# Keeping 32 sample rows in four groups of 32 partitions with 256 columns, from w_out to picking

## The chip, the cores and the metric

The kernel runs on one core of a Trainium2 chip. The metric is the device time of one execution in microseconds (us). Shorter is better. The core's engines are TensorE (PE in the profile, its weight loads PEld), VectorE (DVE), ScalarE (ACT), GpSimd (POOL) and SyncE (SP). SP issues nearly all transfers, on one queue; 16 DMA engines carry them out.

## What is computed

One inference step of a one-layer decoder with 256 prompt rows and 32 sample rows (8 sequences of 4) of 1024 columns, all float32. The part around the change:

```python
merged = (jax.nn.sigmoid(gate_a) * (o_a.astype(x.dtype) @ w_branch_a)
          + jax.nn.sigmoid(gate_b) * (o_b.astype(x.dtype) @ w_branch_b))
x = x + merged @ w_out
h = moe(rmsnorm(x, norm2_w).reshape(B * T, D_MODEL), router_w, router_b,
        expert_w_gu, expert_b_gu, expert_w_down, expert_b_down)
x = x + h.reshape(B, T, D_MODEL).astype(x.dtype)
# moe: logits = x @ router_w + router_b; the 4 best of 32 experts a row, softmax over the 4;
# an expert: h = x @ w_gu + b_gu; act = clamp and SwiGLU of h; out = act @ w_down + b_down
```

Then a final norm of the rows. Every expert's weights are 12 MB (`w_gu` 1024 x 2048, `w_down` 1024 x 1024), and all 32 experts are read.

## The kernel before

**Tiles.** `TILES` (L43) splits the 288 rows in two tiles of 128 prompt rows (0 and 1) and tile 2 with the 32 sample rows. `acc(t)` (L326) says where a tile's rows x stand in PSUM: tiles 0 and 1 in two banks each, 128 partitions by 1024 columns; tile 2 in bank 7, where partition group h (32 partitions) holds columns 256h to 256h+255 of the 32 rows. So the sample rows are in four groups there, but norm, transposes, router and picking of the experts' rows take them as 32 partitions by 1024 columns, from `x2[0:32, 2, :]`.

**Order.** The code writes the order of every engine out by hand, with semaphores between them. The stages around the change:

- SP (L438 to L464) loads the router's weights, the residual rows (`x_sample` as four transfers of 32 rows by 256 columns, L446), the first expert's chunks, `norm2_w` over all partitions (L450, after the wait for `merged` 8), biases, further chunks as their places come free: chunk 6 after the router's first part (`x2T` 4, L458), chunk 7 after w_out (`wo_done` 4), chunk 8 after the last logits, and every later one when the chunk that held its place is used (`w_used`, L466). An expert has six chunks of 2 MB; there are 11 places (`FULL`), in the loop 8 (`WS`).
- PE (L1111 to L1159): `w_out_tile` of tile 2, tile 0, the first half of tile 1; transposes of tile 2 (8, each of 32 rows by 128 columns) and tile 0; the second half of tile 1 in parts, and between these the router (`part_logits`, `fold_logits`, `last_logits`); the ranks of the rows in their experts (`rank`, `total`); then the first expert's picking (L1207), its transposes, and the experts. `keep_busy` issues matmuls whose results nobody reads.
- ACT (L1720, `residual_norm`): sums of squares and 1/rms of each tile. For tile 2 it first copies bank 7 to `x2[0:32, 2, :]` (4 copies), then squares two halves.
- DVE (L2213 to L2292): adds x (`add_x`), scales the rows by 1/rms and `norm2_w`, chooses the experts, makes `sel`, a one-hot matrix of rows by 64 slots; after that the tables for all experts.
- POOL (L2517 to L2551): constants: `ramp`, `fold`, the expert biases in bfloat16, and at its end `same_row`, which sums a column over the four groups; it is used for the final norm at L1398.

**Experts.** For each expert PE runs `gate_up` (L1239), `pick` of the next expert's rows (L1162: rows = sel^T x2, six matmuls of 512 columns, the two of tile 2 with 32 rows), transposes and `down` (L1272); every second expert it adds the outputs to `acc` through `add`. `b_down` (L1185) adds the down bias, once.

Of the kernel before, what the change touches and what calls it, by code (L numbers as in the profile page):

```python
# [27 lines left out]
P = 128  # L28
# [8 lines left out]
D = 1024  # L37
# [39 lines left out]
def layer_kernel(nc, x_prompt, x_sample, state_hgrn, state_rwkv, state_shift, norm1_w, w_in, hgrn_lb_logits,  # L77
# [5 lines left out]
    with ctx:  # L83
# [110 lines left out]
        gselc, selc = ltake(2 * TW), st3[:, 15:18]  # L194
# [26 lines left out]
        same_row = before  # L221
        fold, sq_n = inb[:, 0:NE], qk[:, 0:512]
        part = sk[:, 0:P + NS]
# [5 lines left out]
        bdn = x2[:, 2, :]  # L229
# [6 lines left out]
        sel, gsel = fm[11][:, 0:3 * SLOTS], fm[11][:, 256:256 + 6 * SLOTS]  # L236
# [95 lines left out]
        X2_ORDER = (2, 0, 1)  # L332

# [9 lines left out]
        RR, XX, WO = 7, 7, 4  # L343
# [39 lines left out]
        def _(sp):  # L383
# [72 lines left out]
            for x in range(1, 4):  # L456
                sp.dma_start(bdn[NE * x:NE * x + NE, :], expert_b_down[0]).then_inc(S("bdn_loaded"), 16)
# [61 lines left out]
        def _(pe):  # L519
# [558 lines left out]
            def x2_T(t, out, k0=0, k1=KT):  # L1078

                rows = TILES[t][1]  # L1080
                for k in range(k0, k1):
                    b, c = (out[(k - k0) // 4], (k % 4) * P) if t < 2 else (out[0], k * NS)
                    i = nc.tensor.transpose(b[:, c:c + rows], x2[0:rows, t, k * P:(k + 1) * P], ident[0:rows, 0:rows])
                    if k % 4 == 3 and (t < 2 or k == 7):
                        done(i, "x2T")
# [10 lines left out]
            def fold_logits():  # L1096

                for t, c in ((0, 0), (2, P)):
                    rows = TILES[t][1]
                    i = mm(logit_cols(t)[0:rows, :], part[:, c:c + rows], fold, start=True, stop=True)  # L1100
                done(i, "logits")
# [19 lines left out]
            pe.wait_ge(S("ramp"), 1)  # L1121
# [16 lines left out]
            def rank(t, first=False):  # L1138

                n = TILES[t][1]  # L1140
                return mm(bank[1][:, P + t * NE:P + (t + 1) * NE], before[0:n, :], M[0:n, t * NE:(t + 1) * NE], start=first, stop=True,
                          skip_group_check=True)
# [42 lines left out]
            def b_down():  # L1185

                for t, (o, rows) in enumerate(TILES):
                    for h, (out, c) in enumerate(acc(t)):
                        r = 32 * (1 + (2 * t + h) % 3)
                        i = mm(out, wT[r:r + NE, o:o + rows], bdn[r:r + NE, c], start=False, stop=True, skip_group_check=True)  # L1190
                return i
# [13 lines left out]
            pe.wait_ge(S("rstd"), 7)  # L1205
            pe.wait_ge(S("sel_ready"), 1)
            for j, b in enumerate((bank[6], bank[0])):  # L1207
                for t, (o, rows) in enumerate(TILES):
                    for h in range(2):
                        c = h * 512 + j * 256  # L1210
                        i = mm(b[64 * h:64 * h + 64, 0:256], sel[0:rows, t * SLOTS:(t + 1) * SLOTS], x2[0:rows, t, c:c + 256],
                               start=(t == 0), stop=(t == 2), skip_group_check=True)
# [69 lines left out]
            def pe_pair(quad, p):  # L1282
# [4 lines left out]
                for x in range(2):  # L1287
# [21 lines left out]
                    if x == 1 and static and quad == 0 and p == 1:  # L1309
                        pe.wait_ge(S("bdn_loaded"), 48)  # L1310
# [86 lines left out]
            pe.wait_ge(S("ramp"), 2)  # L1397
# [5 lines left out]
        def _(act):  # L1403
# [316 lines left out]
            def residual_norm(t, wo):  # L1720
# [25 lines left out]
            def x2_evac(t, n, b, k0):  # L1746
# [4 lines left out]
                else:  # L1751
                    i = fn(x2v[:, :, NP_:NT], b[:, 0:KT * NS].rearrange("p (k t) -> p k t", k=KT), ACT.Copy)
# [8 lines left out]
            done(fn(part, bank[6][:, 0:P + NS], ACT.Copy), "x2T_evac")  # L1761
            residual_norm(1, (3, 4))
            act.wait_ge(S("rstd"), 6)
# [110 lines left out]
        def _(dve):  # L1874
# [327 lines left out]
            def onehot(out, c0, w, slots, weights=None):  # L2202

                for t, (o, rows) in enumerate(TILES):
                    dst, src, s1 = out[0:rows, t * w + c0:t * w + c0 + SLOTS], ramp[0:rows, 0:SLOTS], slots[0:rows, t:t + 1]
                    if weights is None:
                        i = v.tensor_scalar(dst, src, s1, None, ALU.is_equal)
                    else:
                        i = v.tensor_scalar(dst, src, s1, weights[0:rows, t:t + 1], ALU.is_equal, ALU.mult)
# [3 lines left out]
            dve.wait_ge(S("norm_loaded"), 32)  # L2213

            def norm_rows(n, dst, order):

                for x, t in enumerate(order):
                    rows = TILES[t][1]
                    if n == 1:
                        add_x(t, x + 1)  # L2220
                    dve.wait_ge(S("rstd"), 3 * n + x + 1)
                    for out, c in acc(t) if t < 2 else [(x2[0:rows, 2, 0:512], slice(0, 512)), (x2[0:rows, 2, 512:D], slice(512, D))]:
# [356 lines left out]
```

## Time and profile before

| | us |
|---|---|
| median of 3 runs | 1319.13 (1318.65 to 1320.28) |
| the profiled execution | 1319.96 |
| its span in the profile | 1318.2 |
| PE busy | 1286.8 (98%) |
| DVE busy | 374.7 (28%) |
| ACT busy | 241.9 (18%) |
| POOL busy | 53.4 (4%) |

Times in the profile count from the span's start. An instruction's line is the line of the kernel; all of ACT's `activation` calls have one line, L1405, that of a helper, so they are told apart by shape and time. "arena" and "ring" are the two large SBUF areas, "bank" a PSUM bank.
### The profile page before, as it was taken

The page shows a single profiled execution, that of the slowest core. Times are in us where ns is not written, and L with a number is a line of the kernel's source. Part 1 is how long each engine was busy: PE and PEld are TensorE (multiplying, and loading weights), DVE is VectorE, ACT ScalarE, POOL GpSimd, SP SyncE. Part 2 cuts the span into 40 slices and gives each one's busy share as a digit, 9 for nine tenths or more (in the row PEclk, how much of TensorE's full clock was granted, in tenths as well). Part 3 has the DMA queues.
Part 4 walks back from the last instruction along what each step waited for, and adds up shares of the span by engine and source line. Part 5 has one row for each costly group of instructions (what it writes and reads, how often), then busy time and mean ns, then how long its engine had stood idle before and what let it go on. Part 6 is the DMA issues. An engine that isn't in the chain of part 4 may idle for free.

```text
span 1318.2 us, 18429 instructions
## 1 busy us (share of the span) xinstructions
PE 1286.8 (98%) x7369; PEld 614.9 (47%) x7369; DVE 374.7 (28%) x1017; ACT 241.9 (18%) x532; POOL 53.4 (4%) x129
## 2 busy tenths in 40 slices
PE   9999999999999999999999999999999999998987
PEld 6778778888744333333333333333333323232333
DVE  3234756554327121121211212212112111211112
ACT  3143343222122110111101111111101101110102
POOL 5000200000060000000000000000000000000000
PEclk9999999999999999999999999999999999999999
DMA  7635437001878999999999999999999999999996
GB/s 234 171 100 191 134 85 271 33 33 34 320 263 352 429 429 428 429 429 428 418 430 429 429 430 430 430 430 430 430 430 430 429 430 430 430 430 429 428 429 266
DMA packets 72736, 449.40 MB, mean 341 GB/s; under 512 B 14404, under 2 KB 43126, under 8 KB 47880
## 3 DMA queue, kind: packets, MB, share of 16 engines
q1 hardware_dynamic: 67090, 445.72, 82.7%
q10 hardware_dynamic: 5590, 2.88, 0.7%
q8 instruction: 42, 0.69, 0.2%
q14 instruction: 14, 0.11, 0.0%
HBM read 443.82 MB, written 4.76 MB: 340 GB/s over the span
## 4 chain that ended last, share of the span: by engine, by line
PE 78%; DMA 17%; DVE 2%; ACT 1%; issue 0%; POOL 0%; SPq 0%; DVEq 0%; POOLq 0%; ACTq 0%
PE bank L1258 25%; PE bank L1278 13%; DMA ring<-in_expert_w_gu_dram 7%; PE bank L559 7%; PE bank L649 5%; PE bank L1166 5%; DMA arena<-in_expert_w_gu_dram 5%; PE bank L1197 4%; DMA extra<-in_expert_w_down_dram 3%; DMA extra<-in_expert_w_gu_dram 2%; PE bank L1073 2%; PE bank L1047 2%; PE bank L940 2%; ACT arena L1405 1%; PE bank L1173 1%; PE bank L923 1%
## 5 line engine op out<-in xcount | busy, mean ns | idle before, releaser
L1258 PE MATMUL bank<-arena 128*64 128x512 f32 x960 | 216.6, 594 | 2.2 <-DMA arena<-in_expert_w_gu_dram 2.2
L1405 ACT ACTIVATE arena<-bank 128x512 f32<-128x512 f32 (+6 forms) x232 | 115.2, 515 | 484.0 <-PE bank L1278 195.9
L1258 PE MATMUL bank<-ring,arena 128*64 128x512 f32 x848 | 189.7, 594 | 3.8 <-DMA ring<-in_expert_w_gu_dram 3.8
L1405 ACT ACTIVATE arena<-arena 128x256 f32<-128x256 f32 (+7 forms) x124 | 68.9, 564 | 470.8 <-DVE arena L2353 463.6
L2353 DVE TENSOR_SCALAR arena<-bank 128x256 f32<-128x256 f32 x64 | 27.0, 422 | 378.9 <-PE bank L1258 378.9
L1258 PEld LDWEIGHTS bank<-arena 128*64 128x64 f32 x960 | 67.2, 137 | 135.7 <-issue 116.9
L1258 PEld LDWEIGHTS bank<-ring,arena 128*64 128x64 f32 x848 | 59.5, 137 | 116.0 <-issue 100.2
L2403 DVE COPY arena<-bank 64x512 f32<-64x512 f32 x30 | 20.8, 694 | 319.6 <-PE bank L1278 319.6
L1278 PE MATMUL bank<-arena 128*64 128x512 f32 x448 | 100.6, 595 | 0.0
L1278 PE MATMUL bank<-ring,arena 128*64 128x512 f32 x448 | 99.7, 595 | 0.0
L1166 PE MATMUL bank<-arena 128*64 128x512 f32 x372 | 89.6, 599 | 0.0
L559 PE MATMUL bank<-arena,ring 128*128 128x296 f32 (+1 forms) x352 | 87.6, 411 | 0.0
L559 PEld LDWEIGHTS bank<-arena,ring 128*128 128x128 f32 x352 | 66.7, 190 | 19.9
L649 PE MATMUL bank<-arena,ring 128*128 128x288 f32 x256 | 75.5, 419 | 0.0
L1197 PE MATMUL bank<-arena 128*32 128x256 f32 (+1 forms) x252 | 66.3, 491 | 0.0
L1278 PEld LDWEIGHTS bank<-ring,arena 128*64 128x64 f32 x448 | 31.2, 137 | 59.5 <-issue 58.2
L1278 PEld LDWEIGHTS bank<-arena 128*64 128x64 f32 x448 | 31.0, 137 | 58.3 <-issue 58.1
L1258 PE MATMUL bank<-extra,arena 128*64 128x512 f32 x240 | 54.5, 596 | 3.7 <-DMA extra<-in_expert_w_gu_dram 3.7
L1166 PEld LDWEIGHTS bank<-arena 128*64 128x64 f32 x372 | 23.8, 134 | 60.6 <-issue 60.6
L1405 ACT ACTIVATE ring<-bank 128x512 f32<-128x512 f32 (+8 forms) x94 | 31.8, 382 | 95.2 <-PE bank L559 50.6
L649 PEld LDWEIGHTS bank<-arena,ring 128*128 128x128 f32 x256 | 44.0, 190 | 10.7 <-issue 2.4
L1197 PEld LDWEIGHTS bank<-arena 128*32 128x32 f32 (+1 forms) x252 | 24.7, 148 | 34.4 <-issue 34.4
(372 smaller groups left out, 1129.5 us busy)
## 6 DMA issues: line engine op xcount, KB each, us to landing
arena<-in_expert_w_gu_dram SPq DMA_DIRECT2D x60, 2048.0 KB, 24.0
ring<-in_expert_w_gu_dram SPq DMA_DIRECT2D x53, 2048.0 KB, 21.5
arena<-in_expert_w_down_dram SPq DMA_DIRECT2D x28, 2048.0 KB, 26.8
ring<-in_expert_w_down_dram SPq DMA_DIRECT2D x28, 2048.0 KB, 21.6
extra<-in_expert_w_gu_dram SPq DMA_DIRECT2D x15, 2048.0 KB, 23.7
ring<-in_w_in_dram SPq DMA_DIRECT2D x23, 1024.0 KB, 5.5
extra<-in_expert_w_down_dram SPq DMA_DIRECT2D x7, 2048.0 KB, 31.8
ring<-in_w_out_dram SPq DMA_DIRECT2D x4, 1024.0 KB, 7.5
```

Source lines behind the costliest of these rows:

```text
L559: i = mm(b[:, 0:cols], slot[:, kt, j * P:(j + 1) * P], xv[:, kt, 0:cols], start=(kt == 0), stop=(kt == KT - 1))
L649: i = mm(bank[g % 2][:, 0:NT], slot[:, kt, (g % 2) * P:(g % 2 + 1) * P], xv[:, kt, 0:NT], start=(kt == 0), stop=(kt == KT - 1))
L940: i = mm(bank[6 - 4 * x][:, (hh % 2) * P:(hh % 2 + 1) * P], Pm, (zaT if lev > 3 else yaT)[:, hh * P:(hh + 1) * P], start=True, stop=True)
L1047: i = mm(bank[n % 2][:, 0:NT], slot[:, kt % 2, j * P:(j + 1) * P], (obT if br else oaT)[:, kt * NT:(kt + 1) * NT], start=(kt == 0), stop=( ...
L1073: i = mm(out, mT[:, kt * NT + o:kt * NT + o + rows], slot[:, kt % 2, c], start=(kt == 0), stop=True, skip_group_check=True)
L1166: i = mm(bank[6][64 * h:64 * h + 64, :], sel[0:rows, t * SLOTS:(t + 1) * SLOTS], x2[0:rows, t, h * 512:(h + 1) * 512], start=(t == 0), sto ...
L1197: return mm(out, GT[:, o:o + rows], yo[:, c], start=False, stop=True, skip_group_check=True)
L1258: ins = mm(bank[q % 2][64 * (q // 2):64 * (q // 2) + 64, :], gu_lhs(c), w[:, q * 512:(q + 1) * 512], start=(c == 0), stop=(c == KT - 1), s ...
L1278: ins = mm(b[64 * h:64 * h + 64, :], lhs(j, r), w[:, r * D + h * 512:r * D + (h + 1) * 512], start=(j == 0 and r == 0), stop=(j == DN - 1 ...
L1405: return nc.scalar.activation(out, in_, f, **kw)
L2353: v.tensor_scalar(by_row(glu, b), gu_half(b, 0), LIMIT, None, ALU.min).then_inc(S("glu_ready"), 1)
L2403: v.tensor_copy(yo[64 * x:64 * x + 64, 512:1024], bank[1][64:128, :]).then_inc(S("y_evac"), 1)
```

## The change

The sample rows stay as they are in bank 7, as 128 partitions by 256 columns, through norm, transposes, router and picking. `norm2_w` is loaded a second time in that layout (`norm2_q`, four transfers). The sum of squares of a row is now the sum over four partitions, made by a matmul with `same_row`. Router logits, choice and ranks of the sample rows are worked out in all four groups at once, and picking uses a one-hot matrix `sel4` with one block of 64 columns per group. The bias matmuls `b_down` are cut by columns of 256 in the same way.

```diff
-        same_row = before
+        norm2_q, same_row, before_s = x2[:, 2, 512:768], x2[:, 2, 768:896], x2[0:NS, 2, 896:1024]
-        bdn = x2[:, 2, :]
+        bdn = x2[:, 2, 256:512]
+        sel, sel4, gsel = fm[11][:, 0:2 * SLOTS], norm2_q, fm[11][:, 256:256 + 6 * SLOTS]
@@ SP, behind the loads of x_sample
+            for h in range(4):
+                sp.dma_start(norm2_q[NS * h:NS * h + NS, :], norm2_w[0, h * 256:(h + 1) * 256].partition_broadcast(NS)).then_inc(S("norm_loaded"), 16)
             w_load(sp, 0, 0)
             w_load(sp, 0, 4)
@@ SP
-            for x in range(1, 4):
-                sp.dma_start(bdn[NE * x:NE * x + NE, :], expert_b_down[0]).then_inc(S("bdn_loaded"), 16)
+            for x in range(4):
+                sp.dma_start(bdn[NE * x:NE * x + NE, :], expert_b_down[0][:, x * 256:(x + 1) * 256]).then_inc(S("bdn_loaded"), 16)
@@ PE, x2_T
-                    b, c = (out[(k - k0) // 4], (k % 4) * P) if t < 2 else (out[0], k * NS)
-                    i = nc.tensor.transpose(b[:, c:c + rows], x2[0:rows, t, k * P:(k + 1) * P], ident[0:rows, 0:rows])
+                    b, c = out[(k - k0) // 4], (k % 4) * P
+                    i = nc.tensor.transpose(b[:, c:c + P], x2[:, t, k * P:(k + 1) * P], ident)
@@ PE
             w_out_tile(2, acc(2))
-            w_out_tile(0, acc(0))
+            w_out_tile(0, acc(0), 0, 4)
+            pe.wait_ge(S("ramp"), 1)
+            pe.wait_ge(S("rstd"), 4)
+            done(mm(bank[6][:, 0:1], same_row, st3[:, 4:5], start=True, stop=True), "ranks")
+            w_out_tile(0, acc(0), 4, KT)
             w_out_tile(1, acc(1)[0:1])
             pe.wait_ge(S("xn_done"), 4)
-            x2_T(2, bank[6:7])
+            x2_T(2, bank[6:7], 0, 2)
...
-            pe.wait_ge(S("ramp"), 1)
             pe.wait_ge(S("x2T_evac"), 3)
@@ PE, pick
-                for t, (o, rows) in enumerate(TILES):
+                for t in range(2):
                     for h in range(2):
-                        i = mm(bank[6][64 * h:64 * h + 64, :], sel[0:rows, t * SLOTS:(t + 1) * SLOTS],
-                               x2[0:rows, t, h * 512:(h + 1) * 512], start=(t == 0), stop=(t == 2), skip_group_check=True)
+                        mm(bank[6][64 * h:64 * h + 64, :], sel[:, t * SLOTS:(t + 1) * SLOTS], x2[:, t, h * 512:(h + 1) * 512],
+                           start=(t == 0), stop=False, skip_group_check=True)
+                for g in (0, 2, 1, 3):
+                    h = g // 2
+                    i = mm(bank[6][64 * h:64 * h + 64, g % 2 * 256:g % 2 * 256 + 256], sel4[:, g * SLOTS:(g + 1) * SLOTS], x2[:, 2, 0:256],
+                           start=False, stop=True, skip_group_check=True)
@@ ACT, residual_norm of tile 2
-                    for out, c in acc(t):
-                        i = fn(x2[r, 2, c], out, ACT.Copy)
-                    done_wait(act, i, "act_step")
-                    halves = [x2[r, 2, h * 512:(h + 1) * 512] for h in range(2)]
+                    done(fn(sq_n[:, 0:256], bank[7][:, 0:256], ACT.Square, accum_out=st3[:, 4:5]), "rstd")
+                    act.wait_ge(S("ranks"), 1)
+                    done_wait(act, fn(st3[:, 11:12], bank[6][:, 0:1], ACT.Ln, scale=1.0 / D, bias=epsc[:, 0:1]), "act_step")
+                    done(fn(st3[:, 14:15], st3[:, 11:12], ACT.Exp, scale=-0.5), "rstd")
+                    return
@@ ACT, behind part_logits
-            done(fn(part, bank[6][:, 0:P + NS], ACT.Copy), "x2T_evac")
+            fn(part[:, 0:P], bank[6][:, 0:P], ACT.Copy)
+            done(fn(part[:, P:2 * P].rearrange("p (a j) -> p a j", a=4), bcast(bank[6][:, P:P + NS].unsqueeze(1), [P, 4, NS]), ACT.Copy), "x2T_evac")
@@ DVE
-            dve.wait_ge(S("norm_loaded"), 32)
+            dve.wait_ge(S("norm_loaded"), 32 + 64)
...
-            norm_rows(1, x2, X2_ORDER[0:2])
+            add_x(2, 1)
+            add_x(0, 2)
+            dve.wait_ge(S("rstd"), 5)
+            step(v.scalar_tensor_tensor(out=x2[:, 2, 0:256], in0=bank[7][:, 0:256], scalar=st3[:, 14:15], in1=norm2_q, op0=ALU.mult, op1=ALU.mult),
+                 "xn_done")
+            dve.wait_ge(S("rstd"), 6)
...
-            for t, (o, rows) in enumerate(TILES):
-                i = v.tensor_scalar(sel[0:rows, t * SLOTS:(t + 1) * SLOTS], ramp[0:rows, 0:SLOTS], 1.0, selc[0:rows, t:t + 1], ALU.add, ALU.is_equal)
-            step(i, "sel_ready")
+            for t in range(2):
+                v.tensor_scalar(sel[:, t * SLOTS:(t + 1) * SLOTS], ramp[:, 0:SLOTS], 1.0, selc[:, t:t + 1], ALU.add, ALU.is_equal)
+            step(v.scalar_tensor_tensor(out=sel4_g, in0=bcast(ramp[:, 1:SLOTS + 1].unsqueeze(1), [P, 4, SLOTS]), scalar=selc[:, 2:3],
+                                        in1=bcast(gmask.unsqueeze(2), [P, 4, SLOTS]), op0=ALU.is_equal, op1=ALU.mult), "sel_ready")
@@ POOL, ahead of ramp64 and "ramp"
-            step(g.memset(lg, 0.0))
-            step(g.memset(Rk, 0.0))
+            for x in range(4):
+                r = slice(NS * x, NS * x + NS)
+                step(g.tensor_copy(same_row[r, :].rearrange("p (a j) -> p a j", a=4), bcast(ident[r, r].unsqueeze(1), [NS, 4, NS])))
+            step(g.memset(gmask, 0.0))
+            for x in range(4):
+                step(g.memset(gmask[NS * x:NS * x + NS, x:x + 1], 1.0))
+            step(g.tensor_copy(before_s.rearrange("p (a j) -> p a j", a=4), bcast(before[0:NS, 0:NS].unsqueeze(1), [NS, 4, NS])))
```

In the same way the first expert's picking (L1207) takes tile 2 as `sel4` blocks with `x2[:, 2, 0:256]`, one matmul of 256 columns where one of 256 columns with 32 rows stood. In the loop, the third of the three one-hot instructions of `onehot` (L2202) writes 256 columns in place of 64. `b_down` has 12 matmuls of 256 columns in two passes with a wait between them, where there were 8 (four of 512 columns and four of 256). The four copies that made `same_row` go from POOL's end.

## Rows read from the trace of the kernel before

**Rows 1.** The page: busy tenths of the DMA engines in 40 slices.
```profile
DMA  7635437001878999999999999999999999999996
```

**Rows 2.** The chain of waits near the end: start us, us, what.
```profile
997.64 31.86 DMA arena<-in_expert_w_gu_dram
...
1264.40 35.15 DMA extra<-in_expert_w_down_dram
...
1299.68 7.13 PE bank L1353 x64
```

**Rows 3.** Stretches: start:end, length, busy by engine, clock, DMA share, GB/s.
```profile
385.00:393.00 8.00, 8.00 (x47) 4.05 (x49) 1.39 (x2) 1.47 (x3) 7.79 (x4) 1.00 0.08 15
...
412.00:413.00 1.00, 1.00 (x16) 0.31 (x16) 0.90 (x4) 0.46 (x1) 0.00 (x0) 1.00 0.00 0
413.00:414.00 1.00, 1.00 (x26) 0.47 (x18) 0.93 (x3) 0.00 (x0) 0.00 (x0) 1.00 0.71 147
...
1220.00:1270.00 50.00, 45.94 (x217) 15.05 (x215) 8.85 (x31) 4.56 (x9) 0.00 (x0) 1.00 1.01 429
```

**Rows 4.** SP's queue in order of time: start us, us, instruction.
```profile
412.81 0.33 SPq L310 DMA_DIRECT2D arena<-in_expert_w_down_dram  x1
```

**Rows 5.** The chain of waits from 362 to 417 us, three of its pieces.
```profile
362.36 24.39 PE bank L1073 x112
386.75 1.63 PE bank L1083 x16
...
404.94 3.28 PE bank L1211 x24
```

**Rows 6.** Norm of tile 2, DVE and ACT in order of time.
```profile
372.51 0.43 DVE L2231 TENSOR_TENSOR bank<-bank,arena 128x256 f32<-128x256 f32 x1 [9.10 <-DMA arena<-in_norm_w_dram]
...
372.97 1.53 ACT L1405 ACTIVATE arena<-bank 32x256 f32<-32x256 f32 x4 [29.33 <-DVE bank L2231]
...
376.86 3.04 DVE L2223 SCALAR_TENSOR_TENSOR arena<-arena 32x512 f32<-32x512 f32 x2 [3.92 <-ACT arena L1405]
```

**Rows 7.** PE in order of time, from 372.8 us: the 128-column w_out matmuls.
```profile
372.42 7.46 PE L1073 MATMUL bank<-ring,arena 128*128 128x512 f32 x17
```

**Rows 8.** The final norm of tile 2: square, its sum, the `same_row` matmul, the next matmul.
```profile
1309.49 0.38 ACT L1405 ACTIVATE arena<-bank 128x256 f32<-128x256 f32 x1
1309.77 0.20 ACT L1405 ACTIVATION_READ_ACCUMULATOR arena<-bank 128x1 f32 x1
...
1310.20 0.28 PE L1398 MATMUL bank<-arena 128*128 128x1 f32 x2
1310.34 0.68 PE L1197 MATMUL bank<-arena 128*128 128x512 f32 x1
```

**Rows 9.** SP's queue, the small loads ahead of the first chunks, and `norm2_w`.
```profile
352.82 3.55 SPq L446 DMA_DIRECT2D arena<-in_x_sample_dram  x4
356.42 0.42 SPq L310 DMA_DIRECT2D arena<-in_expert_w_gu_dram  x1
...
363.43 0.33 SPq L450 DMA_DIRECT2D arena<-in_norm_w_dram  x1
```

**Rows 10.** POOL in order of time: `ramp`'s last instruction, the copies to `same_row`.
```profile
367.36 0.39 POOL L2531 TENSOR_SCALAR arena<-arena 128x64 f32<-128x64 f32 x1
...
404.42 1.38 POOL L2550 COPY arena<-arena 32x128 f32<-32x128 f32 x4
```

**Rows 11.** PE's weight loads in picking: the first expert's, then one in the loop.
```profile
405.96 0.19 PEld L1211 LDWEIGHTS bank<-arena 32*64 32x64 f32 x4 [0.39 <-issue]
...
919.11 0.14 PEld L1166 LDWEIGHTS bank<-arena 128*64 128x64 f32 x2 [0.28 <-issue]
920.06 0.19 PEld L1166 LDWEIGHTS bank<-arena 32*64 32x64 f32 x4 [0.81 <-issue]
```

**Rows 12.** DVE in order of time: the first `sel`; a three-operand instruction on 256 columns.
```profile
404.19 0.61 DVE L2288 TENSOR_SCALAR arena<-arena 128x64 f32<-128x64 f32 x3
...
424.47 0.43 DVE L2357 SCALAR_TENSOR_TENSOR arena<-arena 128x256 f32<-128x256 f32 x1
```

More of the change, by code:

```diff
@@ L1098, in fold_logits @@
                 for t, c in ((0, 0), (2, P)):
-                    rows = TILES[t][1]
-                    i = mm(logit_cols(t)[0:rows, :], part[:, c:c + rows], fold, start=True, stop=True)
+                    i = mm(logit_cols(t), part[:, c:c + P], fold, start=True, stop=True)
                 done(i, "logits")
@@ L1185, in b_down @@
             def b_down():
-                for t, (o, rows) in enumerate(TILES):
[L1188 to L1191, printed above, removed]
+                for x in range(2):
+                    if x:
+                        pe.wait_ge(S("ranks"), 3)
+                    for t, (o, rows) in enumerate(TILES):
+                        for g in (x, 2 + x):
+                            r = slice(NE * g, NE * g + NE)
+                            out = acc(t)[g // 2][0][:, x * 256:x * 256 + 256] if t < 2 else acc(t)[g][0]
+                            i = mm(out, wT[r, o:o + rows], bdn[r, :], start=False, stop=True, skip_group_check=True)
+                    if x == 0:
+                        done(i, "ranks")
             def add_half(t, h):
@@ L2202, in onehot @@
             def onehot(out, c0, w, slots, weights=None):
[L2204 to L2207, printed above, removed]
-                    else:
-                        i = v.tensor_scalar(dst, src, s1, weights[0:rows, t:t + 1], ALU.is_equal, ALU.mult)
-                return i
-            dve.wait_ge(S("norm_loaded"), 32)
[L2215 to L2222, printed above, removed]
-                        i = v.scalar_tensor_tensor(out=dst[0:rows, t, c], in0=out, scalar=st3[0:rows, 12 + t:13 + t],
-                                                   in1=norm2_bc[0:rows, c], op0=ALU.mult, op1=ALU.mult)
-                    step(i, "xn_done")
+                for t in range(3):
+                    src, s1 = ramp[:, 0:SLOTS], slots[:, t:t + 1]
+                    if weights is not None:
+                        i = v.tensor_scalar(out[:, t * w + c0:t * w + c0 + SLOTS], src, s1, weights[:, t:t + 1], ALU.is_equal, ALU.mult)
+                    elif t < 2:
+                        v.tensor_scalar(out[:, t * w + c0:t * w + c0 + SLOTS], src, s1, None, ALU.is_equal)
+                    else:
+                        i = v.scalar_tensor_tensor(out=sel4_g, in0=bcast(src.unsqueeze(1), [P, 4, SLOTS]), scalar=s1,
+                                                   in1=bcast(gmask.unsqueeze(2), [P, 4, SLOTS]), op0=ALU.is_equal, op1=ALU.mult)
+                return i
+            dve.wait_ge(S("norm_loaded"), 32 + 64)
             def add_x(t, wo):
@@ L2272, in _ @@
             choose(0)
-            dve.wait_ge(S("rstd"), 6)
+            dve.wait_ge(S("rstd"), 7)
             dve.wait_ge(S("logits"), 2)
@@ L2544, in _ @@
             pool.wait_ge(S("logits"), 2)
-            pool.wait_ge(S("ranks"), 1)
+            pool.wait_ge(S("ranks"), 2)
             for x in range(3):
                 step(g.memset(rb_bc[0:1, 0:1], 0.0), "y_evac" if x else "gt_evac")
-            for x in range(4):
-                r = slice(NS * x, NS * x + NS)
-                step(g.tensor_copy(same_row[r, :].rearrange("p (a j) -> p a j", a=4), bcast(ident[r, r].unsqueeze(1), [NS, 4, NS])),
-                     "ramp" if x == 3 else "pool_step")
 _INS = ("x_prompt", "x_sample", "state_hgrn", "state_rwkv", "state_shift", "norm1_w", "w_in", "hgrn_lb_logits", "hgrn_gnorm_w",
```

55 lines of the change are left out of this document (27 added, 28 removed).

## The prediction

> **What bounds the kernel now.** I read the page first. PE is busy 98% of the span, but the DMA tenths stand at 9 from the thirteenth slice to the last [rows 1], so both could be the limit. The stretches decide it: between 1220 and 1270 us PE is busy 45.94 of 50 us, while the DMA share is 1.01 at 429 GB/s [rows 3]. The chain of waits near the end says the same: long pieces of it are expert chunks in flight, and the last matmuls (L1353) start when a chunk issued 35.15 us earlier has landed [rows 2]. So the end is the end of the stream of expert chunks, plus a tail of 1318.2 - 1299.7 = 18.5 us.
>
> When does that stream last stand still? The DMA share is 0.08 from 385 to 393 us and 0.00 from 412 to 413; in the next microsecond it is 0.71, and it stays full after [rows 3]. What ends the last pause is the load that SP issues at 412.81 [rows 4], which waits for `w_used` 1: PE has used the first expert's first chunk. From there a fixed number of bytes goes at a fixed rate. **So the change is worth what it moves that event**, and work saved later than 413 us is worth nothing as long as the stream does not starve. Up to there, the chain of waits is PE nearly throughout: 24.39 us of w_out, 1.63 of transposes, 3.28 of picking [rows 5]. A shift of PE anywhere on that way goes one for one into the end, and a saving on ACT or DVE beside it does not.
>
> **What is removed beside PE.** The four copies on ACT (1.53 us) and the slow scaling of tile 2 on DVE (3.04 us, to 379.90) [rows 6] are what the change most visibly takes away. PE asks for that result at 386.7 [rows 5], 6.8 us after it is there. They are worth 0. The new order (DVE adds x to tile 0 first, then scales tile 2 in one instruction of about 0.43 us [rows 12]) stays well inside these 6.8 us.
>
> **The new wait inside w_out (the main cost).** PE now stops after the first 16 of 32 pieces of tile 0, for the square sum of tile 2. When would it be there? Pieces of 512 columns follow each other at (7.46 - 0.59)/16 = 0.43 us, taking 0.59 for the last one's own length (my reading of the row; two passes per matmul) [rows 7]. The transposes come at 386.75 [rows 5]; 32 pieces back (16 of tile 0, 16 of tile 1) is 373.0, and the piece that starts next to it in the sequence of [rows 7] starts at 372.85. When is the sum ready? `add_x` of tile 2 ends at 372.51 + 0.43 = 372.94, and ACT starts 0.03 later [rows 6]. The same square stands in the final norm: start 1309.49, sum read by 1309.97, then the `same_row` matmul, and the next matmul at 1310.34, which is 0.85 us from start to next matmul [rows 8]. So PE goes on at 372.97 + 0.85 = 373.82, not 372.85: **+0.97 us**. Behind the waiting instruction on PE is all of the rest of w_out, so ACT's and DVE's work on tiles 0 and 1 moves with it and hides nothing.
>
> **Later `norm2_w`.** DVE's addition at 372.51 was itself ended by the load of `norm2_w` (9.10 us of waiting) [rows 6]. The four new loads are issued ahead of the chunks that go ahead of `norm2_w`. Call s how much later `norm2_w` lands. At 0.42 us an issue, as the chunk behind them takes, SP reaches the chunks 1.7 us later; at the rate of the four loads of `x_sample`, which have the same size, 3.55 us later [rows 9]. `norm2_w` itself waits for `merged` until 363.43 either way, so s comes only from idle DMA engines before the chunks and from the new bytes: 0.13 MB at 429 GB/s is 0.3 us. Low end 0 (all in gaps), high end 3.55 + 0.3 = 3.9. The transfers of residual rows issued just before still keep the engines busy for a part of the 1.7 us, so I take the value nearer the low end, **+0.7 us**; it is added in full, since PE waits for the addition.
>
> The Trainium skill, page "DMA: Bandwidth & Descriptors", section "Rules for kernel authors", speaks against these four loads: under 64 KB a transfer is mostly overhead, and it should be one large one. Taken as serial overhead that rule gives the high end, while the 0.42 us issues give the lower value; the sum here uses neither but the rows.
>
> **Shorter transposes.** 16 pieces (8 of 32 rows, 8 full) take 1.63 us [rows 5]. At the pace of [rows 7], 128 columns take 0.107 us; ten full transposes take 1.07, and I add 0.1 for the start: 1.17, **-0.46 us**. Bounds: 0 (if a piece has a floor that fills it) and -0.6.
>
> **The first picking.** 24 pieces of 256 columns, two side by side, would take 24 x 0.107 = 2.57 us at that pace; they take 3.28 [rows 5], of which the last piece's end is about 0.3. Where the loads go from 128 to 32 rows and back, PE stands: in the loop a pair of full-row loads starts at 919.11 and the next loads, with 32 rows, at 920.06, which is two steps of 0.43 us and 0.09 more (a load no longer goes a step ahead of its matmul), so 0.09 us a switch [rows 11]. `sel4` has 128 rows, and four switches go: **-0.4 us**, between -0.2 and -0.6. (The Trainium skill, page "TensorEngine Tiling (Array Packing)", section "Key Properties", states that a change of tiling mode drains the engine. The trace agrees, with 0.09 us; by this rule each later pick of the loop gains 0.2 us also, which is a rival below.)
>
> **Small terms.** `sel`: three instructions take 0.61 us; the third becomes one of 256 columns, 0.43 in place of 0.2; one small instruction of the pair before it goes: **+0.1** [rows 12]. Logits of tile 2 with 128 rows and the second copy of `part`: 0 to +0.2, I take **+0.1**; the copy runs under w_out. POOL: `ramp` is ready at 367.75; the copies to `same_row` (1.38), five memsets and a copy more, two memsets less, are about +2 us, so 369.8, 3 us before PE asks for it [rows 10]; 0. The later bias work on POOL waits for its own load. `b_down` stands at some 508 us, `onehot`'s 0.2 us more an expert on a DVE that is busy 8.85 of 50 us [rows 3]: behind the last pause, 0.
>
> **Sum:** 0.97 + 0.7 - 0.46 - 0.4 + 0.1 + 0.1 = **+1.0 us**. On the profiled execution, 1319.96 (span 1318.2 and 1.8 around it), that is 1321.0. This execution was 0.8 above the median of 1319.13, so the median becomes **1320.1**. The bounds of the terms give -0.1 to +5.0.
>
> **Rivals.** (a) *The small loads hold the chunks back.* Place: SP's queue from 356 us. If they go at the pace of `x_sample`, s is 3.9 and the sum is +4.2: 1323.3. It decides from s = 2.4, where the sum passes 0.2% (2.6 us). For it: 3.55 us for four equal loads [rows 9]. Against it: `norm2_w` is issued 7 us behind the chunks, and nothing shows SP blocked at 356.42. (b) *PE is the limit.* 31 picks at -0.2 us are -6 us, partly given back by a new start of each 256-column piece: 1314 to 1316. For it: PE is busy 98% of the span. Against it: PE is idle 4 of 50 us late while the DMA share is 1.01 [rows 3]. (c) *The wait costs nothing*, because the sum is there before PE, as if `norm2_w` landed a microsecond earlier: -0.46 - 0.4 + 0.2 = -0.7, 1318.5. Against it: [rows 6] give no such early landing, and the new loads only add to the queue. (d) *The new needs of `ramp` bite*: POOL late by over 3 us; worked out above at 3 us to spare.
>
> **Chances.** What a measurement of this kernel can tell from no change is about 0.2%, 2.6 us. My forecast (+0.2 to +2.4): 0.70. (a) and (d) above 2.6 us: 0.13. (c): 0.11. (b): 0.06. So faster 0.06, within 0.2% 0.81, slower 0.13. The range reaches from (c), less a little spread of the runs, to the middle of (a): 1318.2 to 1322.8.
>
> **What would show it.** In the changed profile: a gap of PE near 372.9 us inside L1073's work, ended by ACT, about 1.7 us until w_out goes on; `norm2_w` landing after 372.5 but before 374; transposes of tile 2 in two full pieces; no gap of 0.81 us in PEld within a pick; SP's first `w_used` load at about 413.8 and a full DMA share from there; PE idle a little more late in the run. The forecast is wrong if the `w_used` event moves by one amount and the end by another, if the gap is above 3.4 us (a) or absent (c), or if late pauses of PE do not grow though picks got shorter (b).

## The result: same time, 1.0015 of before

| | us | runs | ratio to before, 95% interval |
|---|---|---|---|
| before, beside it | 1318.80 (1318.51 to 1320.28) | 12 | |
| changed kernel | 1320.69 (1319.14 to 1324.65) | 12 | 1.0015 [1.0008, 1.0022] |
| profiled executions | 1319.96 before, 1320.43 after | | spans 1318.2 and 1318.4 |

The forecast of 1320.1 is 0.6 us low, and the time lies inside the range. As a change it is 0.9 low: +1.0 was forecast and the medians are 1.9 apart (+1.1 to +2.9 by the interval of the ratio). The increase is small, but its interval excludes no change. The page of the changed kernel: PE has 4.1 us less work over the run, and the DMA tenths differ from [rows 1] by one step in three slices (the 9th, 12th and 13th).

```profile
PE 1282.7 (97%) x7497; PEld 627.7 (48%) x7497; DVE 379.9 (29%) x1014; ACT 239.5 (18%) x526; POOL 53.3 (4%) x133
...
DMA  7635437011869999999999999999999999999996
```

The chain of waits of the changed kernel (start us, us, what), for the stretch of [rows 5]. Lines have moved: w_out is L1074 here, the `same_row` matmul L1114, the first picking L1222 and L1226.

```profile
363.27 10.12 DMA arena<-in_norm_w_dram
373.47 0.44 DVE bank L2238
373.94 0.48 ACT arena L1419 x2
374.56 0.35 PE bank L1114 x2
374.91 13.84 PE bank L1074 x32
388.75 1.09 PE bank L1083 x10
...
406.48 1.08 PE bank L1222 x8
407.56 0.43 PE bank L1226 x4
408.00 0.86 PE bank L1222 x8
408.86 0.45 PE bank L1226 x4
```

Before, this chain went through PE without a break. Now it leaves PE at 363.27 for the load of `norm2_w`, and comes back by DVE and ACT at 374.56. PE in order of time shows the same as a pause of 1.71 us inside w_out:

```profile
374.56 0.35 PE L1114 MATMUL bank<-arena 128*128 128x1 f32 x2 [1.71 <-ACT arena L1419]
374.77 1.53 PE L1074 MATMUL bank<-ring,arena 128*128 128x512 f32 x3
```

SP's queue in the changed kernel: the four loads, the two chunks behind them, the load that ends the pause at 413, and one at 655 that matters below.

```profile
356.05 1.81 SPq L447 DMA_DIRECT2D arena<-in_norm_w_dram  x4
357.90 0.42 SPq L311 DMA_DIRECT2D arena<-in_expert_w_gu_dram  x1
...
413.89 0.33 SPq L311 DMA_DIRECT2D arena<-in_expert_w_down_dram  x1
...
655.29 0.33 SPq L311 DMA_DIRECT2D arena<-in_expert_w_gu_dram  x1
```

From starts in the two traces, the way to `w_used` 1 splits into: transposes of tile 2 begin at 388.75 in place of 386.75 (+2.00); they take 1.09 in place of 1.63 (-0.54); from their end to the first picking +0.08; from there to SP's load 7.41 in place of 7.87 (-0.46). The load moves from 412.81 [rows 4] to 413.89, +1.08. These times count from the span's start, and w_out itself began 0.15 us earlier in the changed profile (362.21 against 362.36). From the start of w_out the load comes after 51.68 us in place of 50.45, which is +1.23.

**A second pause that I had missed.** SP's queue before has a load at 654.58:

```profile
654.58 0.33 SPq L310 DMA_DIRECT2D arena<-in_expert_w_gu_dram  x1
```

It too waits for `w_used`: SP had issued nothing for 11.0 us before it. It lands 8.9 us later, and around it the stream runs short. Stretches of the kernel before (columns as in [rows 3]): 377 GB/s where 429 is the full rate, which is 8 x (1 - 377/429) = 0.97 us lost. The page of the kernel before has it too, not in its tenths but in its row of GB/s: 418 in the 20th slice, between 428 and 430.

```profile
GB/s 234 171 100 191 134 85 271 33 33 34 320 263 352 429 429 428 429 429 428 418 430 429 429 430 430 430 430 430 430 430 430 429 430 430 430 430 429 428 429 266
...
652.00:656.00 4.00, 4.00 (x20) 1.29 (x18) 0.00 (x0) 0.00 (x0) 0.00 (x0) 1.00 0.96 377
656.00:660.00 4.00, 4.00 (x21) 1.40 (x19) 1.34 (x5) 0.94 (x2) 0.00 (x0) 1.00 0.91 377
```

So PE's work of the nine pickings between 413 and 655 counts as well. There the change gives 0.13 us a picking: a piece of the chain goes from 2.76 us to 2.63 (425.50 to 428.13, where ACT reads the bank). `b_down` takes 3.36 - 2.48 = 0.88 us more, start to the next matmul. PE in order of time, before and then after:

```profile
508.64 2.54 PE L1190 MATMUL bank<-arena 32*128 32x512 f32 x16
511.12 0.66 PE L1173 MATMUL bank<-arena 128*128 128x128 f32 x4
```

```profile
509.18 3.43 PE L1200 MATMUL bank<-arena 32*128 32x256 f32 x24
512.54 0.66 PE L1179 MATMUL bank<-arena 128*128 128x128 f32 x4
```

Together -9 x 0.13 + 0.88 = -0.29; the traces have -0.37, from +1.08 at 413 to +0.71 at 655.

### The profile page after: what moved, and what is told of

Same layout as the page of the kernel before. It is cut to its first block, busy times and chain, and to the rows that moved or that the text cites. A ratio compares the mean times of both kernels' runs of the same rounds, so it can differ in the third digit from the quotient of the medians.

```text
span 1318.4 us, 18684 instructions
## 1 busy us (share of the span) xinstructions
PE 1282.7 (97%) x7497; PEld 627.7 (48%) x7497; DVE 379.9 (29%) x1014; ACT 239.5 (18%) x526; POOL 53.3 (4%) x133
## 4 chain that ended last, share of the span: by engine, by line
PE 77%; DMA 18%; DVE 2%; ACT 1%; issue 0%; SPq 0%; DVEq 0%; ACTq 0%
PE bank L1273 25%; PE bank L1293 13%; DMA ring<-in_expert_w_gu_dram 7%; PE bank L560 7%; PE bank L650 5%; DMA arena<-in_expert_w_gu_dram 5%; PE bank L1208 4%; PE bank L1168 3%; DMA extra<-in_expert_w_down_dram 3%; DMA extra<-in_expert_w_gu_dram 2%; PE bank L1048 2%; PE bank L941 2%; PE bank L1172 2%; PE bank L1074 2%; ACT arena L1419 1%; PE bank L1179 1%
## 5 line engine op out<-in xcount | busy, mean ns | idle before, releaser
L1273 PE MATMUL bank<-arena 128*64 128x512 f32 x960 | 216.6, 594 | 2.1 <-DMA arena<-in_expert_w_gu_dram 2.1
L1419 ACT ACTIVATE arena<-bank 128x512 f32<-128x512 f32 (+7 forms) x230 | 114.4, 516 | 484.0 <-PE bank L1293 195.9
L1419 ACT ACTIVATE arena<-arena 128x256 f32<-128x256 f32 (+8 forms) x121 | 67.4, 565 | 472.5 <-DVE arena L2365 465.4
L1273 PEld LDWEIGHTS bank<-arena 128*64 128x64 f32 x960 | 67.2, 137 | 135.6 <-issue 116.6
L1293 PE MATMUL bank<-arena 128*64 128x512 f32 x448 | 100.6, 595 | 0.0
L1293 PEld LDWEIGHTS bank<-arena 128*64 128x64 f32 x448 | 30.9, 137 | 58.3 <-issue 58.1
L1168 PE MATMUL bank<-arena 128*64 128x512 f32 x248 | 58.5, 592 | 0.0
L1168 PEld LDWEIGHTS bank<-arena 128*64 128x64 f32 x248 | 17.8, 137 | 35.4 <-issue 35.2
```

The lines of the kernel that those rows point to most:

```text
L1168: mm(bank[6][64 * h:64 * h + 64, :], sel[:, t * SLOTS:(t + 1) * SLOTS], x2[:, t, h * 512:(h + 1) * 512], start=(t == 0), stop=False, skip_ ...
L1273: ins = mm(bank[q % 2][64 * (q // 2):64 * (q // 2) + 64, :], gu_lhs(c), w[:, q * 512:(q + 1) * 512], start=(c == 0), stop=(c == KT - 1), s ...
L1293: ins = mm(b[64 * h:64 * h + 64, :], lhs(j, r), w[:, r * D + h * 512:r * D + (h + 1) * 512], start=(j == 0 and r == 0), stop=(j == DN - 1 ...
L1419: return nc.scalar.activation(out, in_, f, **kw)
```

## The experiments

Theory 1: the extra microsecond at `norm2_w` comes from the four small loads ahead of the chunks. It was split later into 1a (their bytes or their issues) and 1b (the landing scatters whatever is ahead of it; only the new wait makes PE feel it). Theory 2: up to 655 us PE's work moves the end, after it PE's work is worth nothing. "Ratio" is to the kernel before on the same chip, with its 95% interval.

### 1. The wait for `norm2_w` moved behind the additions

```diff
-            dve.wait_ge(S("norm_loaded"), 32 + 64)
             add_x(2, 1)
             add_x(0, 2)
+            dve.wait_ge(S("norm_loaded"), 32 + 64)
```

> The changed kernel, with DVE's wait for norm2_w moved behind the two additions of x that don't need it. Theory 1 (only the moment of the first w_used event counts, and PE's pause at 372.9 is a wait for norm2_w through DVE and ACT): the pause of 1.71 us goes, the same_row matmul costs 0.1 to 0.3 us, w_out goes on at about 373.1 in place of 374.77, SP's load behind w_used 1 moves from 413.89 to about 412.2, and the median falls by 1.6 us from that of the changed kernel, to about 1318.2 to 1319.1, at or a little below the kernel before. Rival (the pause isn't norm2_w but the chain DVE, ACT, or ramp from POOL): most of the pause stays, and the time stays near 1320.7.

Measured: 1319.08 (1318.42 to 1319.93), ratio 0.9998 [0.9989, 1.0007]. Nothing in `add_x` reads `norm2_w`, so DVE adds at 365.78, and PE does not stop (PE, then SP, in order of time):

```profile
372.52 0.28 PE L1114 MATMUL bank<-arena 128*128 128x1 f32 x2
372.66 2.82 PE L1074 MATMUL bank<-ring,arena 128*128 128x512 f32 x6
```

```profile
411.78 0.33 SPq L311 DMA_DIRECT2D arena<-in_expert_w_down_dram  x1
```

Without the wait the new layout reaches `w_used` 1 earlier than the kernel before: 411.78 - 362.03 = 49.75 us from the start of w_out, against 412.81 - 362.36 = 50.45 before and 51.68 in the changed kernel. The pause is what the change costs.

### 2. The four loads behind the chunks and behind `norm2_w`

```diff
-            for h in range(4):
-                sp.dma_start(norm2_q[...], norm2_w[...]...)   # ahead of w_load(sp, 0, 0)
+            for h in range(4):
+                sp.dma_start(norm2_q[...], norm2_w[...]...)   # behind the braw loads
```

> The changed kernel, with the four loads of norm2_q behind those of norm2_w and of the gate-up biases, on a semaphore of their own that DVE waits for only ahead of tile 2's scaling. Theory 1 (the four loads ahead of the chunks delayed norm2_w by 0.96 us): DVE's addition goes back from 373.47 to about 372.5, the pause of PE shrinks from 1.71 to about 0.8 us, the w_used load comes at about 412.9, time about 1.0 us below the changed kernel. Rival (that 0.96 us is the spread of the transfers and has nothing to do with the four loads): the addition stays at 373.3 to 373.6 and the time at about 1320.7.

The four loads also have a semaphore of their own, for which DVE waits just ahead of the scaling of tile 2; ahead of the additions it waits for `norm2_w` alone.

Measured: 1321.18 (1319.85 to 1323.61), ratio 1.0014 [1.0005, 1.0023]. The chunks leave at 355.88, 2 us earlier than in the changed kernel, and DVE still gets `norm2_w` only for 373.36:

```profile
373.36 0.43 DVE L2238 TENSOR_TENSOR bank<-bank,arena 128x256 f32<-128x256 f32 x1 [10.14 <-DMA arena<-in_norm_w_dram]
```

The place of the four loads is not the cause.

### 3. Tile 0's pair of matmuls twice in every picking of the loop

```diff
-                for t in range(2):
+                for t in (0, 0, 1):
```

> The changed kernel, with the two matmuls of tile 0 issued twice in every pick of the loop (the second pair starts the sum anew). That is 0.86 us more PE work an expert, some 27 us in all, all behind the last pause of the stream. Theory 1 (the stream of chunks sets the end): nothing, 1320.0 to 1321.5; PE's period of an expert grows from 27.3 to about 28.2 us, still under the 29.3 us that an expert's 12 MB take, and the late waits of PE for chunks shrink. Rival (PE's work sets the end): about +25 us, 1345.

Measured: 1329.51 (1326.55 to 1332.18), ratio 1.0075 [1.0062, 1.0089]. I had expected 413 us to be the last pause; this fell here. PE does 0.86 us more an expert, and the stream stands for long stretches that were full before:

```profile
634.00:642.00 8.00, 8.00 (x40) 2.56 (x38) 3.60 (x14) 0.59 (x1) 0.00 (x0) 1.00 0.51 172
...
660.00:664.00 4.00, 4.00 (x22) 1.43 (x20) 0.00 (x0) 0.00 (x0) 0.00 (x0) 1.00 0.49 152
```

### 4. Eight small matmuls that keep PE busy ahead of the wait

```diff
             pe.wait_ge(S("ramp"), 1)
+            keep_busy(8, bank[6])
             pe.wait_ge(S("rstd"), 4)
```

> The changed kernel, with eight matmuls of 128 columns (1.7 us) whose results nobody reads ahead of PE's wait for the square sum, so that PE isn't idle there. Theory 1: the wait's end doesn't move, time as the changed kernel, 0 to +0.3 us. Theory K (some executions of the changed kernel are 2 to 4 us longer at a lower granted clock, three of twelve, because PE's pause lowers the clock there): the long ones vanish, the highest of five stays below 1321.5, the median falls by up to 0.8 us. Rival of K (they have another source): runs above 1322 go on appearing, about one in four.

Measured: 1320.56 (1320.18 to 1322.88), ratio 1.001 [1.0001, 1.0019]. PE is busy through the old gap, w_out goes on at 374.71 in place of 374.77, and the highest run is still 1322.88, with 2 of 11 above 1322. In the changed kernel's profile the granted clock stays at 1.00 from 372 to 376 us, through the pause. So a clock that falls in the pause is not the cause of the median. For the very longest runs it is not settled. The five runs above 1323.2 us of the changed kernel and of experiments 2 and 5 have a mean granted clock of 0.996 or 0.997, against 0.998 or 0.999 for the other 29 runs of these kernels. None of the 11 runs here is that long, which by the rate of the others (5 of 34) could be chance, and no trace of such a run was kept.

### 5. The four loads left out

The scaling of tile 2 reads memory without `norm2_w` in it, so the sample rows' values are not the reference's; all instructions but the four loads are there, and DVE waits for `norm2_w` alone. Another choice of experts could have brought other work, but PE has 7497 instructions as in the changed kernel.

```diff
-            for h in range(4):
-                sp.dma_start(norm2_q[...], norm2_w[...]...)
```

> The changed kernel without the four loads of norm2_q (left out: the sample rows are scaled with whatever stands there, so their values, their experts and the outputs of all that follows differ) and with DVE waiting for norm2_w alone. What differs from the changed kernel is those four loads. Theory 1a (the four loads delay norm2_w, by up to 1 us): norm2_w has landed by 372.5, the time is about 0.7 to 1.0 us below the changed kernel, near 1319.8, with a narrow spread. Theory 1b (the landing of norm2_w scatters by a microsecond from execution to execution whatever stands ahead of it, and the new wait puts this scatter on PE's path): the time stays within 0.4 us of the changed kernel and the runs go on spreading over 2 us or more. As the choice of experts changes, an additional quad of blocks could run; the block count is read off the trace before the time is.

Measured: 1321.34 (1319.36 to 1323.73), ratio 1.0015 [1.0006, 1.0024]. With no such load at all, PE stops as long (PE in order of time):

```profile
374.47 0.35 PE L1112 MATMUL bank<-arena 128*128 128x1 f32 x2 [1.66 <-ACT arena L1417]
```

1a falls. By the DMA records, the last piece of `norm2_w` lands in the 14 profiled executions of this study between 372.2 and 374.5 us: 372.43 before, 373.39 after, 373.31 here, and 374.51 in experiment 10, whose kernel has none of the four loads either. The profile of before happened to have an early one, and I read its 372.51 as fixed.

How the scatter reaches the stream can be read off the profiles of all kernels with the new layout and the wait. In the changed kernel SP's load near 413 goes 40.50 us after the landing (413.89 - 373.39). In experiments 2, 3, 5, 6 and 7 this is 40.50 or 40.51 again, while the landings lie between 372.22 and 374.16; with the extra matmuls of experiment 4 it is 40.64. The landing moves the load one for one. The latest is that of experiment 7 (chain of waits; its load goes at 414.66):

```profile
363.48 10.68 DMA arena<-in_norm_w_dram
```

### 6 and 7. The doubled picking in the first eight experts only, or in the others only

```diff
-                    pick()
+                    pick(static)       # 6; in 7: pick(not static), and pick(True) in pe_last
```

> The changed kernel, with the two matmuls of tile 0 issued twice in the picks of the first eight experts alone (0.86 us more PE work each, 6.9 us by the eighth). Theory 2 (the stream stands still a last time at about 655 us, where SP's places go from eleven to eight, so PE's pace over the first eight experts counts in full and later pace doesn't): 6 to 8 us longer than the changed kernel, 1327 to 1329. Rival (the double pick's cost comes from all 32 experts, by PE against the stream late in the run): about a quarter of the 9 us measured with all picks doubled, 1323.

> The changed kernel, with the two matmuls of tile 0 issued twice in the picks from the ninth expert on (0.86 us each, 19 to 20 us in all). Theory 2: PE's slack against the stream takes it nearly all; 0 to +2 us on the changed kernel (PE has 1.1 us an expert left in the loop, and the tail after the last chunk is the same). Rival: three quarters of the 9 us, about 1327.

Measured: the first eight, 1326.00 (1325.24 to 1331.56), ratio 1.0064 [1.0044, 1.0084]; the others, 1321.07 (1319.92 to 1324.43), ratio 1.0016 [1.0007, 1.0026], as the changed kernel itself. SP's load at 655 in the first:

```profile
661.00 0.33 SPq L311 DMA_DIRECT2D arena<-in_expert_w_gu_dram  x1
```

Some 6.9 us of PE's work (8 x 0.86) put among the first eight experts cost 5.3 us of the end by the medians (1326.0 - 1320.7, a little under the 6 to 8 expected), 6.5 by the ratios (0.0049). In the profile the stretch from the load at 413 to that at 655 grows from 241.40 to 248.27 us, by 6.87: all of the added work. Nearly three times as much in the other experts costs 0.4 and 0.1, though one of these pickings, the ninth, still lies ahead of the load at 655 (242.27 us). This is Theory 2.

### 8. The bias matmuls moved from the fourth expert to the 29th, on top of 1

The condition taken away holds in the second expert of the second pair, the fourth; where the recorded expectations say "third", it is this one.

```diff
-                    if x == 1 and static and quad == 0 and p == 1:
+                    if x == 0 and bias:        # pe_pair(last, 0, True)
                         pe.wait_ge(S("bdn_loaded"), 64)
                         b_down()
```

> The changed kernel with DVE's wait moved as before (norm_wait_later), and b_down moved from the third expert (512 us) to the 29th. Theory 2: the 3.3 us of b_down go from PE's way to the pause at 655 us to a place where PE waits for chunks anyway; the pause of 1 us there goes, and the time falls by 0.8 to 1.2 us from that of norm_wait_later (1319.08), to about 1318.0, below the kernel before. Rival (only the pause at 413 us counts): no difference, 1319.1.

Measured: 1318.75 (1318.25 to 1318.91), ratio 0.9992 [0.9983, 1.0001]. The median is not the 1318.0 expected, but against the kernel before it is 0.0006, 0.8 us, below experiment 1. The intervals of the two overlap. The same 3.4 us of work now lie where PE has pauses (PE, then SP, in order of time), and SP's load goes at 650.43 in place of 653.18:

```profile
1215.54 3.43 PE L1200 MATMUL bank<-arena 32*128 32x256 f32 x24
```

```profile
650.43 3.76 SPq L311 DMA_DIRECT2D arena<-in_expert_w_gu_dram  x2
```

### 9. The kernel before, with the new wait alone

```diff
-            w_out_tile(0, acc(0))
+            w_out_tile(0, acc(0), 0, 4)
+            pe.wait_ge(S("x_added"), 1)
+            w_out_tile(0, acc(0), 4, KT)
```

> The kernel before, with one dependency of the change added and nothing else: after the first 16 pieces of tile 0's w_out product TensorE waits until VectorE has added x, which itself waits for norm2_w. Theory 1b (the landing of norm2_w scatters by some 2 us whatever is ahead of it, and this wait puts that scatter on TensorE's path): in a profile where norm2_w lands at 372.4 the pause is 0.1 to 0.3 us, in one where it lands at 373.3 to 374.2 it is 1 to 2 us; the median lies 0.3 to 1.0 us over before (1319.3 to 1320.5) and the highest runs above 1321.5. Rival (the scatter doesn't reach the end, the time of the changed kernel comes from its small matmuls and copies): no change of the median, and no wider spread than before.

Measured: 1321.71 (1318.96 to 1322.80), ratio 1.0013 [1.0004, 1.0022]. By the medians that is +2.6 us and by the ratio +1.7, more than the +0.3 to +1.0 that I gave it, though PE's pause in this profile is only 0.81 us (the landing is at 373.77). The chain of waits shows the way of the changed kernel, without `same_row` and ACT in it:

```profile
363.95 9.82 DMA arena<-in_norm_w_dram
373.85 0.44 DVE bank L2233
374.34 14.00 PE bank L1073 x32
```

Old layout, no small loads, no new matmul: the dependency alone brings the time and the spread of the changed kernel. The load at 413 is 1.59 later than in the profile of before, that at 655 1.60, the span 1.8. Not all of it is the wait: w_out began 0.53 later in this profile (362.89 against 362.36), so that from its start the load is 1.06 later (51.51 us against 50.45).

### 10. The kernel before, with the bias matmuls at the 29th expert

The edit is that of experiment 8, with `bdn_loaded` at 48.

> The kernel before, with the 24 bias matmuls and their part of tile 0 moved from the third expert to the 29th. Theory 2 (the stream's last pause is the one at 655, so TensorE's work of the first eight experts counts): the pause of 1.1 us at 655 goes, the load that waited behind w_used there is issued some 3 us earlier than at 654.58, and the time falls by 0.5 to 1.0 us (1318.0 to 1318.5). Rival (the stream decides from 413 on, as I predicted): 0.0 us, within 0.2 of before.

Measured: 1318.91 (1318.07 to 1320.61), ratio 0.9995 [0.9986, 1.0004]. The pause at 655 goes as expected, with the load at 652.47:

```profile
652.00:656.00 4.00, 4.00 (x21) 1.21 (x16) 0.09 (x1) 0.09 (x1) 0.00 (x0) 1.00 1.03 438
656.00:660.00 4.00, 4.00 (x21) 1.48 (x21) 1.25 (x5) 0.86 (x2) 0.00 (x0) 1.00 0.97 414
```

The gain of 0.5 to 1.0 us does not show: -0.2 us is inside the interval. This profile's span is 0.7 above before's, but its execution, 1320.61, is the slowest of the eleven. Inconclusive.

### 11 and 12. Experiments 8 and 1 again, beside 9 and 10

> The changed kernel with both edits, the later wait for norm2_w and the bias at the 29th expert, beside the other three on one chip. Theory 2: 0.3 to 1.0 us under the kernel with the later wait alone. Against the kernel before with the bias at the 29th expert it shows what the layout itself is worth without its wait: -0.7 to +0.3 us. If it is the fastest of the four and its interval against before ends under 1, it beats both kernels.

> The changed kernel with the later wait for norm2_w alone, again, beside the others: 1318.9 to 1319.3, ratio to before 0.9995 to 1.0003. Theory 1b: no run above 1320.5, since the scatter of norm2_w's landing reaches no engine that decides.

Measured: with both edits 1318.59 (1318.29 to 1322.12), ratio 0.9996 [0.9987, 1.0005]; with the later wait alone 1319.43 (1318.30 to 1320.20), ratio 0.9999 [0.9990, 1.0008]. SP's first load comes 49.75 us after the start of w_out again (411.67 - 361.92). The medians of all runs with both edits and with the later wait alone are 1318.62 (22 runs) and 1319.34 (22 runs), 0.7 us apart, and 0.8 us in the runs here. The intervals of the ratios overlap, so a gain of the later bias is likely but not shown. Both edits stand 0.6 to 1.2 us under the kernel before's medians, but neither interval ends under 1, so that it beats that kernel is not shown; it beats the changed kernel, whose own interval starts at 1.0008.

**All together.** The spread separates the kernels best. Of the 56 runs of kernels in which PE waits on `norm2_w` (the changed one, experiments 2, 4, 5 and 9; 3, 6 and 7 do extra work and are left out), 20 are above 1321.5 us; of the 55 of experiments 1, 8, 10, 11 and 12, one is; of 99 of the kernel before, one. The event at 655 orders the spans, but only roughly. Each row is one execution: that of experiment 1 was the fastest of its eleven, that of experiment 10 the slowest, and that of before 1.2 us above its median of 1318.80. From the load near 413 to the end the span has 904.5 to 905.9 us in all rows with the usual picking, so a difference of a microsecond between two spans says little:

| kernel | `norm2_w` lands | SP's load near 413 | near 655 | span |
|---|---|---|---|---|
| both edits (8; 11) | 373.89; 372.70 | 412.22; 412.17 | 650.43; 650.39 | 1316.7; 1316.9 |
| later wait (1; 12) | 372.37; 372.36 | 411.78; 411.67 | 653.18; 653.08 | 1316.3; 1317.3 |
| before, late bias (10) | 374.51 | 412.99 | 652.47 | 1318.9 |
| before | 372.43 | 412.81 | 654.58 | 1318.2 |
| changed | 373.39 | 413.89 | 655.29 | 1318.4 |
| loads behind (2), loads out (5) | 373.28; 373.31 | 413.78; 413.82 | 655.18; 655.23 | 1319.5; 1319.2 |
| PE busy in the wait (4) | 373.19 | 413.83 | 655.23 | 1319.1 |
| before with wait (9) | 373.77 | 414.40 | 656.18 | 1320.0 |
| later experts doubled (7) | 374.16 | 414.66 | 656.93 | 1319.7 |
| first eight doubled (6) | 372.22 | 412.73 | 661.00 | 1323.2 |
| all doubled (3) | 372.72 | 413.23 | 662.35 | 1324.7 |

Where PE does not wait on `norm2_w`, a late landing does nothing: in the four profiles of experiments 1, 8, 11 and 12 it lies between 372.36 and 373.89, and the load near 413 comes 49.75 or 49.76 us after the start of w_out in all of them.

## Why the prediction was right, and where it was not

**What bounds the kernel, and that only `w_used` counts.** The main step held: PE's shift moves SP's load (+1.08 us against a forecast of +1.0, +1.23 from the start of w_out), and the saved copies of ACT and the faster scaling of DVE bought nothing. "**It stays full after**", however, is wrong. I had looked at 412 to 414 and at 1220 to 1270 [rows 3] and took the stretch between for full from the page's tenths, in which a slice is 33 us wide; a microsecond lost is 3% of it, and only the GB/s row below them shows it. The stream runs short once more near 655, and experiments 3 and 6 show that it counts. From this also "b_down and the loop's pickings behind it: 0" failed. It did little harm here, since the two nearly cancel: -1.17 and +0.88.

**The new wait, +0.97.** w_out goes on 374.77 - 372.85 = 1.92 us later; 373.47 - 372.51 = 0.96 of it is DVE's later addition, and the other 0.96 is this term.

**Later `norm2_w`, +0.7.** The profile has 0.96, so the size was near, but the cause that I gave is refuted: with the loads behind (experiment 2) or gone (5) it is the same. What I took as one number is a landing that scatters by 2 us. Before, DVE took it up and PE never saw it; the wait puts it on PE's path. One profile gives one draw of such a number, and I worked with it as if it were fixed.

**The other terms.** Transposes -0.54 (-0.46 forecast), first picking 3.28 to 2.83 and with what follows it -0.46 (-0.4), the small terms +0.08 (+0.2). The switch of tiling at 0.09 us, read from [rows 11], gave a picking of 1.72 + 0.89 us in the loop where 2.75 stood. As the sum of the terms without the wait I had -0.46 - 0.4 + 0.2 = -0.66; experiments 1 and 12 measure 50.45 - 49.75 = 0.70.

**The rivals.** (a), small loads that hold the chunks back, is refuted: they cost SP 1.81 us of issue and nothing measurable. The rule of the Trainium skill that I weighed there (page "DMA: Bandwidth & Descriptors", section "Rules for kernel authors": under 64 KB a transfer is mostly overhead) is about such loads; experiment 5, which leaves all four out, shows no gain (1.0015 with and without). (b), PE as the limit, is half true: not to the end of the run, but to 655 us, so each of nine pickings counts 0.13 us and not 31 of them 0.2. (c), the wait costs nothing, is what the kernel would be with DVE's wait one step later (experiments 1 and 12). (d) did not come: POOL's `ramp` was ready at 369.6, 3.3 us before PE came to the wait at 372.85.

**How near the number was, and by what luck.** SP's load moved by 1.1 or 1.2 us, near the +1.0 forecast, but the medians moved by 1.9. Part of the nearness of 1320.1 is luck: the three runs that it starts from have a median of 1319.13, 0.3 above that of the twelve. What the remaining 0.7 to 0.8 us between load and medians are is not shown. It lies inside the interval of the ratio (+1.1 to +2.9 us).

**Signs of being wrong that came, and one that did not.** I had written that the forecast is wrong if SP's load moves by one amount and the end by another. In the two profiles the load moved by 1.08 and the span by 0.2. The rest of the span took 904.5 us in place of 905.4, and the table shows that it scatters by more than that, so one pair of profiles cannot decide on this sign. The full DMA share from 413 on did not come either, for the reason given above. I also expected PE to be idle more late in the run. Over the run it is (35.7 us against 31.4, of which 1.7 is the new pause), but between 1220 and 1270 us it is busy 46.55 us, more than the 45.94 of [rows 3]; that single stretch was a poor test, since the pauses move through it.

**Open.** How much of the 1.9 us between the two medians is the wait and how much the layout: the events say +1.93 (51.68 - 49.75) and -0.70 (49.75 - 50.45), together +1.23; the runs of experiments 1 and 12 say that the layout alone is within 0.1% of before. And why experiment 10 gained nothing though its pause at 655 is gone: the stream's own start-up between 413 and 424 us, which differs from profile to profile, may hide it, but no run was made on that. Open as well are the longest runs with their lower granted clock (experiment 4).

## What to carry to other kernels

A wait costs what the thing that it waits for scatters, not only what it shows in one profile: before tying a bounding engine to a load, ask who took up that load's lateness so far. Put a wait in front of the first instruction that reads the data, not in front of the block that holds it; here one moved line is the whole loss. When a kernel is bound by a stream, look for its last pause in the GB/s row of the page and then in stretches of a few microseconds over the whole length, since the tenths do not show one.

## What was not expected of the hardware

- A 512 KB load broadcast over partitions, issued between 363.0 and 364.0 behind transfers in flight, landed 8.9 to 10.9 us later, with a scatter of over 2 us from profile to profile (372.2 to 374.5) and no visible dependence on four loads of 32 KB ahead of it.
- The stream ran short once more 240 us after its start, where SP had waited 11.0 us for a place in SBUF to come free. PE's added work in the eight experts ahead of it was felt for the most part (0.86 x 8 = 6.9 gave 5.3 us), while nearly three times that work later gave 0.4 us.
- Full-row pickings with sample rows as four blocks of 256 columns took 2.61 us in place of 2.75, at a third more matmul instructions.
